# Where the high and low weights lie in SBUF: 448 modulo 512 bytes for both, in a two-layer decoder kernel

## The reference

```python
x = x + mlstm_layer(x, ...)        # rmsnorm, x @ w_in (1024x3080), chunked recurrence, @ w_out
x = x + conv_ffn(x, layer 0)       # rmsnorm, @ w_up (1024x5632), width-3 conv, silu(gate)*val, @ w_down
k_sh, v_sh = shared_kv(x, ...)     # rmsnorm, @ w_kv (1024x6144)
x = x + dilated_attention_layer()  # rmsnorm, @ w_q (1024x3072), 3 groups, softmax, @ w_out
x = x + conv_ffn(x, layer 1)
return rmsnorm(x, final_norm_g)
```

## Time and profile before

| | |
|---|---|
| median of 3 runs | 792.14 us |
| the profiled execution, its own time | 791.78 us |
| its span, first to last instruction | 789.7 us |
| mean granted TensorE clock | 0.993 |
| TensorE matmuls busy | 765.8 us, 97% |
| weight loads busy | 751.4 us, 95% |
| VectorE busy | 535.2 us, 68% |
| ScalarE busy | 458.6 us, 58% |
| GpSimd busy | 226.7 us, 29% |
| read from HBM | 134.54 MB, mean 172 GB/s |

### The profile page before, as it was taken

How to read it: one execution, slowest core, us unless ns; L and a number is a source line. 1 busy time by engine, 2 the same in 40 slices (tenths; PEclk the granted TensorE clock), 3 DMA queues, 4 the chain that set the end, 5 groups by cost and what they waited for, 6 DMA issues and landing times.

```text
span 789.7 us, 17137 instructions
## 1 busy us (share of the span) xinstructions
PE 765.8 (97%) x6534; PEld 751.4 (95%) x6534; DVE 535.2 (68%) x983; ACT 458.6 (58%) x608; POOL 226.7 (29%) x190
## 2 busy tenths in 40 slices
PE   8999989999999999999999999999999999999995
PEld 8989889999999999999999999999998999999995
DVE  5776867888878744646646646565678888788442
ACT  6552546756566546447647746835856665665451
POOL 2520222523422342222222220311232234222331
PEclk9999999999999999999999999999999999999998
DMA  9653426565555566754473374474426655554721
GB/s 293 203 165 107 135 82 212 174 200 190 182 182 184 186 193 205 226 191 141 131 236 128 104 246 149 149 230 139 152 83 201 226 186 187 183 189 147 238 93 53
DMA packets 139804, 136.23 MB, mean 173 GB/s; under 512 B 3585, under 2 KB 139089, under 8 KB 139764
## 3 DMA queue, kind: packets, MB, share of 16 engines
q1 hardware_dynamic: 127968, 130.11, 50.9%
q10 hardware_dynamic: 11796, 5.56, 2.8%
HBM read 134.54 MB, written 1.13 MB: 172 GB/s over the span
## 4 chain that ended last, share of the span: by engine, by line
PE 57%; DVE 22%; issue 10%; ACT 7%; DVEq 1%; DMA 1%; ACTq 0%; POOL 0%; POOLq 0%
DVE wlo L860 8%; PE bank L1315 7%; PE bank L1317 7%; PE bank L1316 7%; PE banks L1315 6%; PE banks L1317 6%; PE banks L1316 6%; PE bank L1539 3%; DVE cb L1107 3%; PE bank L1541 3%; PE bank L1540 3%; PE banks L1601 2%; ACT cb L690 2%; DVE bank L1101 2%; PE banks L1573 2%
## 5 line engine op out<-in xcount | busy, mean ns | idle before, releaser
L471 POOL TENSOR_TENSOR wlo<-raw,whi 128x512 fp32r<-128x512 f32 (+1 forms) x169 | 218.1, 1322 | 526.5 <-ACT whi L512 526.5
L512 ACT ACTIVATE whi<-raw 128x2048 fp32r<-128x2048 f32 (+1 forms) x136 | 238.1, 1751 | 199.2 <-PE bank L1317 106.1
L860 DVE TENSOR_TENSOR wlo<-raw,whi 128x1024 fp32r<-128x1024 f32 x161 | 197.1, 1262 | 15.0 <-ACT whi L512 14.3
L1315 PE MATMUL bank<-xsA,whi 128*128 128x256 f32 x568 | 159.4, 281 | 2.9 <-DVE wlo L937 1.9
L1317 PE MATMUL bank<-xsA,wlo 128*128 128x256 f32 x568 | 157.7, 278 | 0.0
L1316 PE MATMUL bank<-xsA,whi 128*128 128x256 f32 x568 | 157.6, 278 | 0.0
L1315 PE MATMUL bank<-xsB,whi 128*128 128x256 f32 x480 | 134.0, 279 | 0.4 <-DVE cb L1111 0.3
L1317 PE MATMUL bank<-xsB,wlo 128*128 128x256 f32 x480 | 132.6, 276 | 0.0
L1316 PE MATMUL bank<-xsB,whi 128*128 128x256 f32 x480 | 132.6, 276 | 0.0
L1315 PEld LDWEIGHTS bank<-xsA,whi 128*128 128x128 f32 x568 | 107.5, 189 | 4.7 <-issue 3.7
L1316 PEld LDWEIGHTS bank<-xsA,whi 128*128 128x128 f32 x568 | 107.5, 189 | 0.1
(11 more groups left out here) (200 smaller groups left out, 1572.3 us busy)
## 6 DMA issues: line engine op xcount, KB each, us to landing
raw<-in_f_w_up SPq DMA_DIRECT2D x44, 1024.0 KB, 5.1
raw<-in_w_kv SPq DMA_DIRECT2D x24, 1024.0 KB, 5.3
raw<-in_f_w_down SPq DMA_DIRECT2D x16, 1024.0 KB, 5.1
raw<-in_b_w_q SPq DMA_DIRECT2D x12, 1024.0 KB, 5.3
raw<-in_a_w_in SPq DMA_DIRECT2D x10, 1024.0 KB, 5.8
raw<-in_f_w_down SPq DMA_DIRECT2D x8, 768.0 KB, 4.9
Bi<-bias_by_distance ACTq DMA_DIRECT2D x16, 320.0 KB, 4.6
raw<-in_a_w_out SPq DMA_DIRECT2D x4, 1024.0 KB, 5.2
```

Source lines behind the costliest of these rows:

```text
L471: o = g.tensor_tensor(wlo[s][:, ka:kb, :], raw[s][:, ka * CW:kb * CW] .rearrange("p (k c) -> p k c", c=CW), whi[s][:, ka:kb, :].bitcast(F3 ...
L512: o = a.activation(whi[s][:, k0:k1, :], raw[s][:, k0 * CW:k1 * CW] .rearrange("p (k c) -> p k c", c=CW), ACT.Copy)
L860: v.tensor_tensor(wlo[s][:, ka:kb, :], raw[s][:, ka * CW:kb * CW].rearrange("p (k c) -> p k c", c=CW), whi[s][:, ka:kb, :].bitcast(F32), A ...
L1315: t_.matmul(ps, hi_w, hi_x, start=first, stop=False)
```

## The change

Four lines of the allocation change places. `onec`, a column of ones that takes 64 bytes, is placed before `whi` and no longer between `whi` and `wlo`; `wroot`, 64 bytes too, goes behind `wlo`.

```diff
         epsc = place("epsc", [P, 1])
+        onec = place("onec", [P, 1])
         whi = [place(f"whi{s}", [P, KD, CW], F32R) for s in range(RING)]
-        onec = place("onec", [P, 1])
+        wlo = [place(f"wlo{s}", [P, KD, CW], F32R) for s in range(RING)]
         wroot = place("wroot", [P, 1])
-        wlo = [place(f"wlo{s}", [P, KD, CW], F32R) for s in range(RING)]
```

## The result

The changed kernel takes 811.87 us (median of 4 runs, 810.05 to 813.29) where the kernel before takes 792.14 (792.02 to 792.45). The ratio is 1.0251, interval 1.0232 to 1.0269. The forecast was 777 us, so its direction was wrong. The profiled execution took 811.54 us, its span is 809.6.

A forecast was written before the change was run, and what follows sets the result against it. TensorE's matmul count times pace was taken as the bound; 11.7 us (large products) plus 5.2 us (exchanged roles) gave 16.9 us, less a tenth 15.2 us, so 777 us from the median of 792.14, range 765 to 797 us.

The forecast's parts named there:

- What bounds the kernel: Whole kernel: TensorE, busy 765.8 of 789.7 us, sets the time by its number of matmuls and their pace.
- the reading of the list: Paces by address difference modulo 256: 0 the worst at 120 ns, 64 and 192 halfway, 128 the best.
- Rival C: Large and exchanged products: pattern repeats every 128 bytes, so 128 acts like 0, 120 ns; 828 us, chance 0.16.
- The 110 ns of a weight load alone: TensorE's matmuls: a weight load alone needs about 110 ns, to which the streamed read adds 2 to 10 ns.
- Term 1: 5088 large products with stationary weights (L1315 to L1317): 113.3 to 111 ns at difference 128, 11.7 us less.
- Term 2: 768 products with exchanged roles (L1539, L1347 and partners): 117.8 to 111 ns, 5.2 us less.
- Rival A: Only the 768 exchanged products gain, falling to 113.3 ns, 3.5 us less; 788.7 us, chance 0.16.
- The tenth taken off: Whole kernel: a tenth of the 16.9 us gain lost to waits, mostly at the ends, leaving 15.2 us.
- Rival B: Whole kernel: nothing happens, pace does not hang on the pair's addresses modulo 256; 792.1 us, chance 0.16.

The follow-up runs named there:

- both192: Against the kernel before: whi and wlo both at 192 modulo 512 (ident moved from 256 to 320), moving tiles at 64, difference 128; 810.89 us.
- the table: Separate kernel of matmuls alone, without the decoder, run once: sections for all 64 pairs of eight offsets, alternating patterns and 16-byte steps; paces only, 120 ns at difference 0.
- both0: Against the kernel before: whi and wlo both at 0 modulo 512, moving tiles at 64, difference 192; 804.54 us.
- hi384_lo448: Against the kernel before: whi stays at 384, wlo goes to 448 as in the changed kernel, differences 64, 64, 128; 808.84 us.
- hi0_lo384: Against the kernel before: the offsets of whi and wlo exchanged, whi at 0 and wlo at 384, differences 192, 192, 64; 809.24 us.
- shift64: Against the kernel before: all addresses the large products use moved by 64 bytes, whi 448, wlo 64, moving tiles 128, differences 64, 64, 192; 791.61 us.
- both384: Against the kernel before: whi and wlo both at 384 modulo 512, moving tiles at 64, difference 64; 799.39 us.

## Why the prediction was wrong, point by point

- **What bounds the kernel**: right. TensorE's pace times its matmuls is the time, the pace depends on the addresses at full clock, and nothing else moved (converters, gates, `Vs` products). TensorE's idle time did not grow by the forecast 1 to 3 us but fell, from 23.9 to 21.5.
- **The step that failed** is the reading of the list: "If what counts is how far apart the two reads start within 256 bytes, then 0 is the worst, 64 and 192 are halfway on both sides (which agrees with `whi` and `wlo` at one pace), and 128 is as far as one can get." At 128 the pace is 118.9, not 111 (the changed kernel, both192). 0 is the worst, but 128 is next to it, and 64 and 192 are the best, not halfway. The equal paces of `whi` and `wlo` fitted a period of 128 as well, which the text itself said under C; the choice between them was made on a picture of two reads far apart and not on a row. The 110 ns of a weight load alone, on which the picture stood, no run shows either. (The row that gave it is of float32, in a list that is headed fp32r; 0.38 less 0.274 us is 106 ns, and from start to start the trace has 109.)
- **Term 1** was 11.7 us less by the choice of 111 ns; it is 20.1 us more. The bounds of 110 to 120 ns held the 118.9.
- **Term 2**, the exchanged roles: 5.2 us less forecast, 0.1 us more measured; 117.8 went to 118.5 ns. This row was a warning that was read wrongly. At differences 192, 64, 192 it wasn't at 113.3, and I took that as an argument against C. It is the second pace of these pairs. That it is not the first is measured, in the kernel and in the table's alternation, but not explained: with the moving tile at 0 in both0 it came.
- **Rival C** had the direction and the reason: 128 counts nearly like 0. Its size was off: 828 us by 120 ns on all, with nothing hidden. Measured are 118.9 ns, and 6.8 us that do not show, 811.9. And a period of 128 bytes explains neither hi384_lo448 nor hi0_lo384. It had a chance of 0.16, and the range left most of it out.
- **Rival A** looked at the exchanged products. They did not gain here, but both0 shows that they can: 114.9 ns, 96.6 us in all against 98.1.
- **The tenth taken off** for the waits had the right sense; a quarter would have been the right size: 6.8 of 26.9 us, and 1.5 of these came from the clock. The waits shrank in the middle too, not only at the ends.
- **Rival B** fell: by the rule that weight loads take nothing from the running matmul's reads (the Trainium skill, "TensorE: Matmul & The Clock Gate", Part 2, LDWEIGHTS) no order of the allocation would move the time. Shifting tiles by 64 bytes moved it by 2.5% and back (811.87 us, shift64 791.61). Which read or which part of a matmul loses the 5 ns, no run shows.

What stays open: why a steady stream has two paces at one set of offsets, and why 64, 64, 192 always finds back to the fast one when 192, 192, 64 does not. The runs show it; no run here tells what in the reads does it. That the two reads meet in SBUF is the likely cause, and it is only argued: no run took one of the reads away.

## What to carry to other kernels

Where matmuls follow back to back, read the pace from start to start and hold it against pairs of operands at other offsets: 64 bytes of allocation are worth 5% of it. Here the fast pace was kept by differences of 64, 64, 192 bytes modulo 256, with the moving tiles at 64 and at 128 alike; the same differences in another order did not keep it (hi0_lo384). So measure each layout in the kernel itself, and don't infer an untried offset from a picture of the memory. And a pace that has two levels under one pair of addresses cannot be settled by one short run: look for where it changes along the timeline.

## What the runs showed of the hardware that was not expected

- fp32r matmuls of 128 stationary and 256 moving columns at full clock run at 113.3, 117.8, 118.7 or 120 ns by the offsets of their operands and by what interrupted them before, with the same instructions.
- At one pair of offsets the pace can be 113.3 ns for over 20 us or 117.8 for over 100; an interruption changes it (both384 at 213 and 320 us). At other offsets the two are 118.7 and 120 (the changed kernel), or 113.3 and 118.9 (hi0_lo384).
- Differences 64, 64, 192 in this order find back to 113.3 ns within some 13 matmuls of a wait (the kernel before, 213.05 to 214.59 us); no layout with other differences did so in all its longer stretches.
- One matmul in three at difference 128 slows the others (hi384_lo448: two of the three distances are 119.0 and 119.5 ns, where difference 64 alone has 113.3 or 117.8).
